# Two small tables padded to 512 bytes a partition in a two-block transformer kernel

## What is computed

```
mod = jax.nn.silu(c) @ w_mod[l] + b_mod[l]          # w_mod is 2048 x 12288
sh1, sc1, g1, sh2, sc2, g2 = jnp.split(mod[:, None, :], 6, axis=-1)
mod_c = jax.nn.silu(c_ctx) @ w_mod[l] + b_mod[l]
h = modulate(rmsnorm(x, norm1_w[l]), sh1, sc1)
```

```
def block(args):
    hx, ix, gx = args                               # 128 tokens, ix and gx are 128 x 128
    act = jax.nn.gelu(jnp.einsum('td,ted->te', hx, expert_u[ix]).astype(jnp.float32), approximate=False)
    return jnp.einsum('te,ted->td', (gx * act).astype(h.dtype), expert_v[ix])
```

## Time and profile before

| | us |
|---|---|
| median of 3 runs | 3998.22 |
| lowest, highest | 3995.88, 3999.73 |
| profiled execution | 4002.12 |
| its span, first to last instruction | 4000.3 |
| PE / DVE / ACT / POOL busy | 3238.5 / 2427.1 / 1187.9 / 929.5 |
| stage of the experts, with its selection | about 1420 to 2720 |
| mean granted clock of TensorE, of full speed | 0.91 |

### The profile page before, as it was taken

The page is one execution under the profiler, slowest core; times in us unless marked ns, Lnnn a source line. Parts: engine busy times, 40 slices in busy tenths (PEclk is TensorE's granted clock), DMA queues, the critical chain, the costliest instruction groups (busy, mean ns, idle before and its releaser), DMA issues. The chain is left out here.

```text
span 4000.3 us, 39602 instructions
## 1 busy us (share of the span) xinstructions
PE 3238.5 (81%) x14024; PEld 2234.9 (56%) x14024; DVE 2427.1 (61%) x3283; ACT 1187.9 (30%) x1887; POOL 929.5 (23%) x791
## 2 busy tenths in 40 slices
PE   5899998759998928777777877777998778987598
PEld 1588776538797813223322323335886667876587
DVE  1556554658776485566556655546555457869575
ACT  1432122335434401111111111103454244644553
POOL 0000010010000056544554554530001116400010
PEclk8899998869998969999999999998999579998699
DMA  9567322019864479999999999994663034530064
GB/s 355 183 213 285 122 90 85 2 47 360 313 200 147 139 298 422 422 422 422 422 422 422 422 422 422 422 422 132 185 190 116 4 117 145 173 94 4 20 192 146
DMA packets 177323, 941.98 MB, mean 235 GB/s; under 512 B 21528, under 2 KB 26776, under 8 KB 99000
## 3 DMA queue, kind: packets, MB, share of 16 engines
q0 software_dynamic: 82944, 604.02, 36.8%
q1 hardware_dynamic: 94272, 336.67, 25.5%
HBM read 938.51 MB, written 2.10 MB: 235 GB/s over the span
## 5 line engine op out<-in xcount | busy, mean ns | idle before, releaser
L1616 PE MATMUL bank<-pe_v_rows,pe_diag 128*128 128x512 f32 x1920 | 907.3, 621 | 354.5 <-DMA pe_v_rows<-in_expert_v,pe_staged_v 211.6
L1479 DVE SCALAR_TENSOR_TENSOR pe_junk<-pe_u_rows,h_rows 128x2048 f32<-128x2048 f32 x256 | 587.0, 2293 | 459.4 <-DMA pe_u_rows<-in_expert_u,pe_staged_u 448.3
L1616 PEld LDWEIGHTS bank<-pe_v_rows,pe_diag 128*128 128x128 f32 x1920 | 362.2, 197 | 899.0 <-issue 483.6
L1424 POOL DMA_INDIRECT pe_v_rows<-in_expert_v,pe_staged_v x248 | 307.9, 1242 | 359.9 <-PE bank L1616 304.6
L1424 POOL DMA_INDIRECT pe_u_rows<-in_expert_u,pe_staged_u x256 | 335.7, 1311 | 228.3 <-DVE pe_junk L1479 134.4
L1577 ACT ACTIVATE pe_diag<-ident,pe_weights 128x128 f32<-128x128 f32 x240 | 91.6, 399 | 747.5 <-PE bank L1616 747.3
L268 PE MATMUL bank<-h_parts,b_top 128*128 128x512 f32 x768 | 271.3, 399 | 9.2 <-DVE b_rest L369 9.2
L369 DVE TENSOR_TENSOR in_rest<-in_ring,in_top 128x1024 fp32r<-128x1024 f32 x112 | 138.3, 1236 | 221.1 <-ACT in_top L338 221.0
L369 DVE TENSOR_TENSOR c_rest<-c_ring,c_top 128x1024 fp32r<-128x1024 f32 x128 | 176.4, 1385 | 100.5 <-ACT c_top L338 100.2
L369 DVE TENSOR_TENSOR ab_rest<-ab_ring,ab_top 128x1024 fp32r<-128x1024 f32 x112 | 136.9, 1225 | 148.7 <-ACT ab_top L338 148.6
L270 PE MATMUL bank<-h_parts,b_rest 128*128 128x256 f32 x768 | 215.3, 280 | 0.0
(11 more groups left out here) (541 smaller groups left out, 6442.9 us busy)
## 6 DMA issues: line engine op xcount, KB each, us to landing
b_ring<-in_w_mix SPq DMA_DIRECT2D x128, 512.0 KB, 6.3
in_ring<-in_w_in SPq DMA_DIRECT2D x112, 512.0 KB, 3.7
ab_ring<-in_w_ab SPq DMA_DIRECT2D x112, 512.0 KB, 3.8
mod_ring<-in_w_mod SPq DMA_DIRECT2D x32, 1024.0 KB, 8.1
v_rows<-in_w_mod POOLq DMA_DIRECT2D x32, 1024.0 KB, 5.4
k_cols<-in_w_mod POOLq DMA_DIRECT2D x32, 1024.0 KB, 8.3
c_ring<-in_w_c_in SPq DMA_DIRECT2D x64, 512.0 KB, 4.5
c_ring<-in_w_glu_out SPq DMA_DIRECT2D x64, 512.0 KB, 4.3
```

The costliest lines, as they stand in the source:

```text
L1424: gp.indirect_dma_start(buf[:, slot, :], None, table, bass.IndirectOffsetOnAxis(ap=staged[which][:, tile, e:e + 1], axis=0)).then_inc(sems ...
L1479: nc.vector.scalar_tensor_tensor(out=junk[:, :], in0=ub[:, s, :], scalar=1.0, in1=h2tm[:, tile, :], op0=ALU.mult, op1=ALU.mult, accum_out= ...
L1616: mm = nc.tensor.matmul(banks[4 * tile + b][:, :], diag[:, e % 4, :], vb[:, s, b * 512:(b + 1) * 512], start=False, stop=False, skip_group ...
```

## The change

```
--- before.py
+++ after.py
@@ -2733,7 +2733,7 @@
 def consts(nc, st, ctx, t):
     ident = ctx.enter_context(nc.sbuf_tensor("ident", [P, P], F32))
     ones = ctx.enter_context(nc.sbuf_tensor("ones", [P, P], F32))
-    gains = ctx.enter_context(nc.sbuf_tensor("gains", [P, 6, KT], F32))
+    gains = ctx.enter_context(nc.sbuf_tensor("gains", [P, 8, KT], F32))
     with st.stage() as (block, sem):
         const_in = sem("const_in")
 
@@ -2741,7 +2741,7 @@
         def _(sp):
             sp.dma_start(ident[:, :], t["c_ident"]).then_inc(const_in, 16)
             sp.dma_start(ones[:, :], t["c_ones"]).then_inc(const_in, 16)
-            sp.dma_start(gains[:, :, :], t["gains"]).then_inc(const_in, 16)
+            sp.dma_start(gains[:, 0:6, :], t["gains"]).then_inc(const_in, 16)
             sp.wait_ge(const_in, 48)
     return {"ident": ident[:, :], "ones": ones[:, :], "gains": gains}
 
@@ -2846,7 +2846,7 @@
         att = ExitStack()
         with ExitStack() as s1:
             hT = sb("hT", [P, KT, 512], s1)
-            modc = sb("modc", [P, 32, 2], s1)
+            modc = sb("modc", [P, 64, 2], s1)[:, 0:32, :]
             ring = sb("mod_ring", [P, 4, UNIT], s1)
 
             first_gates_and_modulation(st, nc, t, hT, h, ring, banks, modc, c_silu, gate_rows, con)
```

## The result

The changed kernel takes 3980.30 us (median of 6 runs, 3970.72 to 3985.62) against 3998.97 us of before beside it (6 runs, 3993.74 to 4007.45). The ratio is 0.995 with a 95% interval of 0.9933 to 0.9968. The medians are 18.7 us apart, where no change was forecast and 3990 was the lower end of the range.

The account below looks back on a forecast made before the run. The prediction took the experts' stage, bound by its gathers on never-idle DMA engines, as the limit (PE elsewhere). All terms were zero, so the forecast was the median of before, 3998.22 us, with a range of 3990 to 4006.

Parts of the forecast that it names:

- The bound: Experts' stage: lasts as long as its gathers on 16 never-idle DMA engines, 1273 us for all rows; PE has over 300 us left.
- I take zero for the 65536 rows: Experts' gathers: moving the rows' start from 384 to a multiple of 512 saves nothing on 310.8 ns a row.
- The pairs of rings: Other streams: aligned against unaligned ring, 47.4 against 52.4 engine-us per MB alone, 44.3 against 42.8 beside modulation rows.
- the loaded pair: `in_ring` (0) and `b_ring` (384) beside POOL's modulation rows: 44.3 and 42.8 engine-us per MB, taken as no saving from alignment.
- The bound for a saving, 0.1 us a DMA from the landings: Ring streams: most an aligned start could save per 512 KB DMA, from median landings of 3.7 against 3.8 us.
- The first rival: Experts' gathers: a start off the boundary costs each row something, so the change saves 20 to 54 us; chance 0.07.
- Its signs: Experts' slices at 428 GB/s or more, stage 20 to 54 us shorter, DVE's wait less by as much, ring landings changed.
- the prediction's estimate of 20 us from it: Experts' gathers: 260 beats at 384 against 256 at 0, 1.5% of 1273 us, giving 3978 us.
- The second rival: Experts' stage: aligned tiles meet more often in the same part of memory, 3.5% or 45 us slower, 4043 us; chance 0.04.
- The modulation ring at zero: First stage, 32 DMAs of 1 MB: aligning the ring saves zero, or 3 us by the landings' 0.1 us a DMA.
- Compute engines at zero: Casts, subtractions, L1479 and L1616 take the same time at another start; subtractions bounded at 8 us of DVE either way.
- its weak step: Experts' gathers: assumes the full-queue rate doesn't depend on the start, which no pair isolated at same load, packet and source.

Follow-up runs that it names:

- The light runs: Kernel before, rows at 384 or at 0 of 512, dot products cut to 256 of 2048 columns, TensorE to one v-row quarter: 3997.48 and 3981.39 us.
- ring_only: Kernel before with only `modc` padded by 384 bytes, so that `mod_ring` begins at 0 of 512: 3997.86 us, ratio 1.0004.
- light_384: Kernel before, rows still at 384 of 512, dot products on 256 of 2048 columns and TensorE on one quarter of each v row: 3997.48 us.

## Why the prediction was wrong

- **The bound** was read rightly. The experts' stage follows the gathers, what a row costs there reaches the end in full, and PE and DVE had the room that was named. The light runs show it from the other side.
- **"I take zero for the 65536 rows"** is the step that failed: the price of a row's start, where the DMA engines are never idle. The term measures 3.9 ns x 65536 / 16 = 16 us. The pairs of rings in the earlier trace rows could not carry it. The change moved their starts, `in_ring` to 128 and `b_ring` to 0, so the same stretches of after test them. Their q1 rows are, for 150 to 250, 300 to 400 and 900 to 1080 us:

```profile
q1 hardware_dynamic: 5647, 18.72, 55.6%
```

```profile
q1 hardware_dynamic: 2691, 9.53, 26.3%
```

```profile
q1 hardware_dynamic: 9380, 34.12, 50.0%
```

  That is 47.5, 44.2 and 42.2 engine-us per MB, where it was 47.4, 44.3 and 42.8. The differences between the rings stayed with the rings and did not move with the start. Nor could this measure have shown the price. The runs that place these rings as before does give 46.4 to 49.6, 42.7 to 44.8 and 41.7 to 43.2 in the same stretches, a spread of 3.5 to 7%, and the rows' price is 1.3%. The 1.5 between the loaded pair, on which the zero rests, is no more than that spread. The packet records are sharper: the median 4 KB packet of these rings took 159 ns in before and in after, at 0 and at 128 (`in_ring`), at 384 and at 0 (`b_ring`), while the median 8 KB row went from 313 to 309. Even the pair called loaded (DMA shares 0.78 and 0.97) was thus read for a case that it does not stand for. In these runs the cost shows only at share 1.01, with over half of the rows off.
- **The bound for a saving, 0.1 us a DMA from the landings,** was no price but scatter. `in_ring`'s median landing is 3.6 to 4.2 us in the runs that start it where before has it (3.7), and 4.0 in after. The first rival was thus right in that a start off the boundary costs each row something, and was given 7 in 100, with a price of 51 us from rows where 16 came. Its signs, as written, would not have been met either: 427 GB/s and 15.6 us, where 428 or more and 20 to 54 were named. The rule of the Trainium skill's page "DMA: Bandwidth & Descriptors" ("How a descriptor splits into AXI transactions"), by the prediction's estimate of 20 us from it, was closer than any row, in part by luck: that estimate counts beats, and the beats do not give the cost at the other starts. The argument against the rule (the loaded pair) was the weak one.
- **The second rival** (aligned starts collide) is refuted: no kernel with rows on the boundary is slower than before.
- **The modulation ring at zero** was right: ring_only, 1.0004.
- **Compute engines at zero** was right for casts, subtractions, L1479 and L1616. It left out TensorE's streams, whose matmuls were in the profile with other distances of their operands. The change keeps that distance, so the total is hardly touched (L274 395 to 398 ns, L270 287 to 285, about what the unchanged placement gives too: 397 and 285 in light_384); the remark that nearly all distances stay was right, and what was missed is that one of them was a bad one.
- **The range** took the spread of three runs and no unknown, since the unknown had been set to zero. The prediction named as its weak step that no pair isolated the start at the same load, packet and source; a step with that note should have left room for its rival inside the range, and should not have given no change 0.89.

## What to carry to other kernels

Where a stage keeps the DMA engines at a share of 1, put the buffers of its rows on multiples of 256 bytes; 4 ns of 311 is small, but it is on the path for every row. Below that share, or with every other gather on, a start off the boundary costs nothing that shows here. Look at the distance of TensorE's two operands in memory too: a multiple of 256 bytes was worth 1.3 to 2% of a matmul-bound projection. And before a difference between two rows is used as a price, look how far the same row lies apart in two runs of the same placement.

## What was not expected of the hardware

- With half of the rows off the boundary in turn with the others nothing is paid (306.9 to 307.0 ns, and 307.6 in stretches of 64), with all of them off 3.9 ns each, and between the two it grows about in line (308.9 at three quarters).
- With the rows on the boundary 99.9% of their packets took the same 309 ns.
- How far off the boundary a row starts hardly counts: 310.9 ns at 64 and at 128 bytes past it, 312.0 at 32 and at 224.
- The 128x512 matmuls of L274 took 395 to 398 ns with their operands 128 bytes off a multiple of 256 apart, and 389 to 390 ns with a multiple of 256 between them, with both on and with both off the boundary; those of L298 397 to 399 and 394.
